# The even mixer of a two-layer transformer: its gated half's input tiles among the attention's steps

## What is computed

```python
q, k, v, bu, bv = jnp.split(z @ w_in, EVEN_SPLIT, axis=-1)
q = apply_rope_2d(rms_norm(q.reshape(b, s, A_HEADS, HEAD_DIM), q_gain), ang_r, ang_c)
k = apply_rope_2d(rms_norm(k.reshape(b, s, A_KV_HEADS, HEAD_DIM), k_gain), ang_r, ang_c)
...
y = jnp.concatenate([window_gqa(q, k, v, kc, vc, sink),
                     chunk_gmlp(bu, bv, v_gain, ws, bias)], axis=-1) @ w_out

def window_gqa(...):      # blocks of 128 queries; keys: previous, own, next block, and the context
    s_loc = jnp.where(valid, q.k * scale, NEG)
    p = softmax(concatenate([s_loc, s_ctx, s_sink]))
    o = p_loc @ v + p_ctx @ v_ctx

def chunk_gmlp(bu, bv, v_gain, ws, bias):
    u = jax.nn.gelu(bu)
    vv = rms_norm(jax.nn.gelu(bv)..., v_gain)          # per group of 64
    mixed = einsum('gij,bnjgd->bnigd', ws, vv) + bias  # per chunk of 128 tokens
    return u * mixed
```

## Time and profile before

| | us |
|---|---|
| median of 3 runs (3691.76 to 3694.46) | 3692.49 |
| the profiled execution | 3691.06 |
| its span in the profile | 3689.3 |
| its mean granted PE clock | 0.975 of 2.4 GHz |
| PE busy | 3540.4, 96% of the span |
| DVE busy | 2022.8, 55% |
| ACT busy | 983.9, 27% |
| even mixer, start of input tiles to start of output tiles | 630.60 to 993.62 |

### The profile page before, as it was taken

How to read it: one execution, slowest core, us unless ns; L and a number is a source line. 1 busy time by engine, 2 the same in 40 slices (tenths; PEclk the granted TensorE clock), 3 DMA queues, 4 the chain that set the end, 5 groups by cost and what they waited for, 6 DMA issues and landing times.

```text
span 3689.3 us, 45766 instructions
## 1 busy us (share of the span) xinstructions
PE 3540.4 (96%) x19352; PEld 3249.3 (88%) x19352; DVE 2022.8 (55%) x3166; ACT 983.9 (27%) x1442; POOL 18.2 (0%) x36
## 2 busy tenths in 40 slices
PE   6999999988899999999999999899999999999998
PEld 4999999976799999999999999777888878877777
DVE  6666645347657574456454455574333756455554
ACT  5112113134431111132111131443222432332232
POOL 0000000000000000000000000000000000000000
PEclk8999999988999999999999999899999999999999
DMA  5333422100023433113333122002222310111122
GB/s 199 126 126 124 132 70 78 65 12 4 25 68 116 135 115 101 59 65 128 126 123 98 60 98 70 17 34 83 97 96 93 126 57 13 64 67 55 51 91 80
DMA packets 86955, 308.53 MB, mean 84 GB/s; under 512 B 9856, under 2 KB 10048, under 8 KB 86368
## 3 DMA queue, kind: packets, MB, share of 16 engines
q1 hardware_dynamic: 82800, 290.04, 23.6%
q0 software_dynamic: 3952, 15.57, 1.2%
HBM read 301.38 MB, written 4.19 MB: 83 GB/s over the span
## 4 chain that ended last, share of the span: by engine, by line
PE 87%; DVE 8%; ACT 2%; issue 2%; DMA 1%; SPq 0%; ACTq 0%; DVEq 0%
PE psum L362 75%; PE psum L1188 2%; PE psum L1171 2%; PE psum L1179 1%; PE psum L993 1%; DVE nmx L1240 1%; DVE wl L355 1%; PE psum L1006 1%; ACT wh L345 1%; PE psum L2176 1%; PE psum L1728 1%; DVE ev_s L1237 1%; DMA raw<-in_ada_w 0%; PE psum L1737 0%; PE psum L2156 0%
## 5 line engine op out<-in xcount | busy, mean ns | idle before, releaser
L362 PE MATMUL psum<-zh,wh 128*128 128x384 f32 (+2 forms) x3792 | 1136.2, 358 | 33.7 <-DVE wl L355 12.3
L362 PE MATMUL psum<-zh,wl 128*128 128x384 f32 (+2 forms) x3792 | 1116.1, 353 | 0.0
L362 PE MATMUL psum<-zl,wh 128*128 128x384 f32 (+2 forms) x3792 | 1116.1, 353 | 0.0
L362 PEld LDWEIGHTS psum<-zh,wh 128*128 128x128 f32 x3792 | 701.1, 191 | 83.8 <-issue 22.5
L362 PEld LDWEIGHTS psum<-zl,wh 128*128 128x128 f32 x3792 | 702.2, 191 | 42.8 <-issue 4.6
L362 PEld LDWEIGHTS psum<-zh,wl 128*128 128x128 f32 x3792 | 701.2, 190 | 43.5
L345 ACT ACTIVATE wh<-raw 128x1024 fp32r<-128x1024 f32 (+2 forms) x431 | 437.1, 1022 | 978.4 <-PE psum L362 758.4
L355 DVE TENSOR_TENSOR wl<-raw,wh 128x1024 fp32r<-128x1024 f32 (+2 forms) x431 | 509.3, 1182 | 323.6 <-ACT wh L345 322.8
L688 DVE TENSOR_TENSOR scr<-psum,rf 128x768 f32<-128x768 f32 x132 | 126.4, 958 | 415.4 <-PE psum L362 415.4
L362 PE MATMUL psum<-hidh,wh 128*128 128x384 f32 (+1 forms) x1232 | 336.6, 342 | 0.0
L362 PE MATMUL psum<-hidh,wl 128*128 128x384 f32 (+1 forms) x1232 | 336.5, 342 | 0.0
(11 more groups left out here) (359 smaller groups left out, 2839.4 us busy)
## 6 DMA issues: line engine op xcount, KB each, us to landing
raw<-in_wup SPq DMA_DIRECT2D x176, 512.0 KB, 3.3
raw<-in_mod_w SPq DMA_DIRECT2D x128, 512.0 KB, 3.2
raw<-in_wdn SPq DMA_DIRECT2D x64, 448.0 KB, 3.3
raw<-in_w_sw SPq DMA_DIRECT2D x36, 512.0 KB, 3.2
raw<-in_wdn SPq DMA_DIRECT2D x32, 512.0 KB, 4.2
raw<-in_ada_w SPq DMA_DIRECT2D x16, 512.0 KB, 5.4
raw<-in_od_in SPq DMA_DIRECT2D x16, 512.0 KB, 3.2
raw<-in_w_ga SPq DMA_DIRECT2D x16, 512.0 KB, 3.3
```

The lines of the kernel that those rows point to most:

```text
L362: last = nc.tensor.matmul(psum[:, at + to:at + to + e - s], w[:, wslot(n), q * P:(q + 1) * P], x[:, q, s:e], start=(q == 0 and j == 0), st ...
```

## The change

Stage `ev_in` becomes two: `ev_qkv` (k, k, v, q, q, q, q: seven tiles) and `ev_uv` (vv 4, u 4). The seven run as before, with the sums of squares (L1378), the roots and the first rotation in the borders between tiles. The eight others are cut into their 64 chunks. Three or fewer chunks run in each of five turns, beside the remaining rotations, and then one or two after the scores in each step of the attention (`chunks_at`), which ends them in step 30. ACT and DVE do their share (gelu, square, gain, splits; drains, splits) at the same step in their own loops. All of `ev_uv` uses PSUM slot 0 (`alone`).

The query norm is no longer multiplied into q: its factor goes into the exponential as a scale per query row, its gain into the rotation matrix (`permqe`). The masks are added by PE: a product of the identity with `ev_mask` (L1638). DVE takes the maximum straight from PSUM. The lag is 1, there is one score buffer in PSUM and two probability buffers. The attention's output goes back into `ev`, and its high and low parts are made per head pair at the end. vv transposes are in steps 22 to 27, the mixing in steps 32 to 43, half a block at a time with one PSUM buffer (`VV_STEPS`, `MIX_STEPS`). The rows of `ev_out` are turned round so that the gated half comes first.

```diff
+        VV_STEPS = {22 + a: a for a in range(6)}
+        MIX_STEPS = {32 + s: s for s in range(12)}
+        def chunks_at(i):
+            return (1, 2, 1, 2, 2)[(i - 1) % 5] if i else 2
 PE, attention:
+            for i in range(NE + 2):
+                if i < NE:
+                    u = EUNITS[i]
+                    if i:
+                        pe.wait_ge(ea_e, i)
+                    for k, c, w in u.keys:
+                        masks = [m for m in u.masks if c <= m < c + w]
+                        last = nc.tensor.matmul(u.scores(c, w), u.q, k, start=True, stop=not masks)
+                        for m in masks:
+                            last = nc.tensor.matmul(u.scores(m, P), ident[:], ev_mask[:, min(m, P):min(m, P) + P],
+                                                    start=False, stop=True)
+                    last.then_inc(ea_qk, 1)
+                chunks_pe(pe, run, chunks_at(i))
+                if i in VV_STEPS:
+                    vv_rows_pe(pe, VV_STEPS[i])
+                if i in MIX_STEPS:
+                    mix_pe(pe, MIX_STEPS[i])
+                if 1 <= i <= NE:
+                    u = EUNITS[i - 1]
+                    pe.wait_ge(ea_p, i)
...
+                if i >= 2:
+                    u = EUNITS[i - 2]
+                    pe.wait_ge(ea_pc, i - 1)
...
 the mixing products wait for the step before:
+        def mix_pe(pe, s):
...
+            if s:
+                pe.wait_ge(mx_d, s)
 ACT, with a step's chunks:
+        def chunks_act(act, run, count):
+            for k in run.finished():
+                n, row = EU.n[k], ev[:, VVROW + k, :]
+                act.wait_ge(drained, DR[n])
+                if k < 4:
+                    link(act, "act", nc.scalar.activation(row, row, ACT.Gelu_apprx_tanh))
...
+                    nc.scalar.activation(esq[:, k % 2], row, ACT.Square).then_inc(v_sq, 1)
+                    nc.scalar.activation(row, row, ACT.Copy, scale=cols[:, BV + k:BV + k + 1]).then_inc(gelu_done, 1)
...
+            for s, k, q in run.take(count, True):
+                if q == 0:
+                    split_hi(act, s.n[k] + AHEAD)
 DVE, attention:
+            for i in range(NE + 2):
+                drains_dve(dve, run)
+                if i < NE:
...
+                    link(dve, "dve", nc.vector.reduce_max(m, u.scores(u.c0, u.w), AX.X))
+                    nc.vector.tensor_scalar(m, m, er[:, 48 + u.factor:49 + u.factor], nsinks[:, u.hd:u.hd + 1],
+                                            ALU.mult, ALU.min).then_inc(ea_s, 1)
+                if 1 <= i <= NE:
...
+                    nc.vector.tensor_scalar(u.probs(), u.probs(), rinv[:, r], None, ALU.mult).then_inc(ea_p, 1)
...
+                if i - 2 in MIX_STEPS:
+                    mix_low_dve(dve, MIX_STEPS[i - 2])
+                if i - 1 in MIX_STEPS:
+                    mix_dve(dve, MIX_STEPS[i - 1])
...
+                chunks_dve(dve, run, chunks_at(i))
```

More of the change, by code:

```diff
@@ L1286, in even_pool @@
             pool.dma_start(bbias[:], t["bbias"]).then_inc(ev_loaded, 16)
[L1287 removed]
+            pool.wait_ge(n_sum, 2)
             pool.dma_start(ev_mask[:], t["c_ev_mask"]).then_inc(ev_mask_in, 16)
             c_rows_pool(pool, 1)
[L1291 to L1317, removed]
[L1318 to L1321 removed]
@@ new lines, in drains_dve, with chunks_dve @@
+        def drains_dve(dve, run):
+            for k in run.finished():
+                drain_row(dve, EU, EU.n[k], ev[:, VVROW + k])
+                if k == 5:
+                    dve.wait_ge(v_root, 1)
+                    nc.vector.reciprocal(vr[:], vr[:]).then_inc(v_r, 1)
+        def chunks_dve(dve, run, count):
+            for s, k, q in run.take(count, True):
+                if q == 0:
+                    split_lo(dve, s.n[k] + AHEAD)
+                if q == s.chunks - 1:
+                    run.late.append(k)
@@ new lines, in even_dve @@
+            drain_to(dve, EQ, ev, norm=1, then=along)
+            run = Along(EU)
+            for turn in range(EV_TURNS):
+                drains_dve(dve, run)
+                if turn == 0:
+                    k_norm(dve, 1)
+                rope(dve, turn + 1)
+                if turn == 1:
+                    dve.wait_ge(v_tr, 1)
+                    for d in range(2):
+                        last = nc.vector.tensor_copy(vdup[:, :, :, d, :], psum[:, E_VT:E_VT + T]
+                                                     .rearrange("p (a g d) -> p a g d", a=6, g=2))
+                    last.then_inc(v_cp, 1)
+                if 1 <= turn <= 3:
+                    qk_factor(dve, turn + 2)
+                chunks_dve(dve, run, 3)
@@ L1422, in even_dve @@
+            heads_lo(dve, 3)
             dve.wait_ge(mod_done, 12)
@@ L1571, in build @@
         SM = 7
-        class Along:
-            def __init__(self, *stages):
-                self.units = [(s, k, q) for s in stages for k in range(s.tiles) for q in range(s.chunks)]
-                self.at, self.late = 0, []
-            def take(self, count):
-                self.at += count
-                return self.units[self.at - count:self.at]
-            def left(self):
-                return self.at < len(self.units)
         def along_pe(pe, run, count, then=None):
```

509 lines of the change are left out of this document (387 added, 122 removed).

## The result

| | us |
|---|---|
| before, median of 4 runs | 3693.03 |
| after, median of 4 runs | 3770.43 (3768.70 to 3771.62) |
| after / before | 1.0209, 95% interval 1.0197 to 1.0221 |
| span of the profiled execution after | 3766.9 |

The changed kernel is slower by 77 us. The direction was forecast, the size was not: 20 us were forecast, and 3770 lies above the range.

The account below looks back on a forecast made before the run. The prediction took PE to bound the mixer, with serial waits giving back what filling gains: 64.7 + 27 + 168.3 + 103.8 = 363.8 us against 363.0. Clock costs made it +20.8, span 3710, time 3713 us; range 3670 to 3745.

Parts of the forecast that it names:

- gelu steps: Steps 1, 6, 11, 16, 21, 26: PE waits behind ACT's table load, gelu and split and DVE's split; 28.9 us extra.
- mixing wait: Steps 33 to 43: PE's mixing products wait for DVE's product, about 3.5 us in eleven steps.
- ordinary division wait: In ordinary attention steps, transposes of probabilities wait 0.2 to 1.1 us for DVE's division.
- 12 us for six gelu steps: Low PE clock after gelu steps: 2 us each, bounds 0 and 4 (one step's work at half rate).
- 8 for the last 19 steps: Low clock in steps without chunks: 28% of 100 us, PE-bound for 0.3; upper bound all 48 us of PE work twice.
- the rival that the low clock holds in the last 19 steps: Attention's last 19 steps: 48 us of PE work doubled, 40 more than taken, 3753 us; chance 0.10.
- filled steps keep the clock up: Rival: chunks keep PE busy through waits, the 20 us of clock do not come, 3693 us; no change, chance 0.20.
- The masks: Six new mask products per head on PE, 6 x 0.22 = 1.4 us a head.
- Scores and P*V: PE work per attention head at full clock: scores 4.7 us, the 44 records of P*V 4.9 us.
- A chunk: One chunk of a weight tile on PE, priced 110.48/14/8 = 0.99 us.
- The start: Seven q, k, v tiles with borders, 64.7 us, and five turns, 27 us, ahead of the attention.
- The table drain: Rival: each of six table loads on the path also drains about 1.38 us, 8 us more, 3721 us; chance 0.07.

Follow-up runs that it names:

- e6: Changed kernel with vv transposes and mixing products behind P*V on PE, weight split ahead of gelu on ACT, division ahead of drain and maximum on DVE: 3676.4 us.
- e12: Changed kernel with unused PE products: eight of 256 columns behind each of six gelu steps, two of 512 columns in each of steps 32 to 48: 3721.4 us.
- e5: Changed kernel with two unused 512-column fp32 products on PE in each of steps 32 to 48: 3737.8 us.
- e8: Changed kernel with eight unused 256-column fp32 products on PE in each of steps 2, 7, 12, 17, 22 and 27: 3751.4 us.
- e4: Changed kernel without the 48 mask products of the scores on PE: 3742.4 us.
- e11: Changed kernel with a plain copy in place of each of the eight gelus, and the table loads around them gone: 3751.0 us.

## Why the prediction was right and where it was wrong

**The direction and its reason: right.** The prediction said that what filling gains, the serial steps give back. With the three orders changed, +77 us becomes -15 (e6). Each of the three is worth 21 to 32 us by itself, clock included.

**The waits: right in kind, the gelu steps too high.** The mixing wait was forecast about 3.5 us eleven times and is 3.43. The ordinary division wait was forecast 0.2 to 1.1 and is 0.69 where one chunk covers it. The gelu step was forecast at "some 5" and is 3.83 in the step shown, 4.7 at the longest. Its chain from the table load to the end of the split is 767.40 - 761.34 = 6.1 us, as priced (6.6 less the 0.45 of the output copy). The six waits together are 4.24 + 3.83 + 4.39 + 4.71 + 2.79 + 3.20 = 23.2 us, where the sum had 28.9 beyond the ordinary wait: at least 6 too much.

**The clock: the step that failed.** The sum took 12 us for six gelu steps and 8 for the last 19 steps, 20 in all. The runs show 49 us and more: e12 gives 49 back although it does 50 us of work beside, some 9 of them outside the waits. So the low clock's cost is estimated at 49 to 58 us. The mis-sized term was in two places. For the last steps, "28% of their 100 us" was carried over from the attention before, where the waits were 1.4 us. The new steps had waits of 3 us in nine, and the clock was 0.64 and 0.59, so most of the 48 us of PE work ran at half rate. In e5 the same steps have a clock of 0.98. The sum's own bound, "all 48 us of PE work twice", and the rival that the low clock holds in the last 19 steps describe what happened there: e5 gives 33 us back, the rival had 40. The rival's chance was 0.10, and its 3753 falls short too, since it left the gelu steps at 12 us. For the gelu steps, 2 us was taken as half the work of one step. The dip goes on for about ten us after the wait (770 to 780 at 0.50), while PE is busy nearly all the time, and so more than one step's work runs at half rate. e8 finds 19 us and more for six of them, 3 us and more each: inside the bounds of 0 and 4, above the 2 that was taken.

The Trainium skill (TensorE: Matmul & The Clock Gate, section HAM oscillation — how this bites in real kernels) tells of a kernel in which every short burst of products is followed by a wait, there for a DMA, so that each burst starts at the low level again. By that rule, the trace agrees: burst, wait of 3.1 to 3.8 us, burst, at a mean clock of 0.64. The prediction used section What's actually happening of the same page of the Trainium skill, for the rival that filled steps keep the clock up. In steps 0 to 31 PE was shown busy for 176.78 of 208.10 us, 0.85, no more than in the attention before (134.28 of 158.00), and their mean clock is 0.87 where that had 0.86.

**The masks: a second mis-sized term.** 1.4 us a head, priced from rows of products of one kind; they are 2.55 a head at full clock, so 20.4 instead of 11.5 us. The alternation of 64-row and 128-row products was visible in the order of the changed kernel. No row that the prediction used has its price, but the trace of before does: two score records of 256 columns take 0.63 us until the transposes begin, not 0.43.

```profile
850.61 0.70 PE L1171 MATMUL psum<-ev 64*128 64x256 f32 x2
851.24 0.77 PE L1179 MATMUL psum<-ident,ev_s 128*128 128x128 f32 x5
```

**Scores and P*V: a little dear too.** At full clock a head's scores without masks, each up to the chunk that follows, are 1.07 + 1.28 + 1.28 + 1.06 + 0.62 + 0.62 = 5.9 us in e4, where 4.7 was priced. P*V up to the next scores is 0.54, 0.99 and 1.21 us for 4, 8 and 10 records (760.41, 755.84 and 750.27), 5.5 a head against 4.9. That is 1.8 a head, at most 14 us over eight, since some of it can lie under a wait.

**A chunk: wrong by its divisor.** 110.48 us in the earlier trace rows are 624 records, 13 tiles of 48 and not 14, so a chunk is 110.48/13/8 = 1.06 and not 0.99. For 50 chunks in steps 0 to 30 this is 3.5 us.

**The start: 4.7 too long.** The first scores come at 717.62 instead of 722.3. It is the same divisor: eight tiles of 8.50 and not 7.89 leave 54.1 us for the other seven and not 59.0, and the 14 chunks of the turns take 1 us more.

**The table drain: did not happen.** The gelu starts at 762.64, 0.02 us after its load ends (761.34 + 1.28). The Trainium skill (ScalarE: Activation LUTs, section What ACT_TABLE_LOAD costs) adds a drain of about 1.38 us to each switch; no run here shows it. In e11, without the load, the wait is 1.42 us shorter. The load's own 1.28 and the drain of that page of the Trainium skill would together be 2.7, as an estimate.

**The account.** The mixer came out 55.6 us above the forecast of 383.8. The clock is 29 to 38 of it, the masks 9, the chunks 3.5, the start -4.7, the gelu waits -6. That makes 31 to 40. The scores and P*V can give up to 14 of the 16 to 25 us that are left, which was not tested alone; the rest is not assigned. Two of the errors pull the other way, 11 us together, and by luck hid as much of the others.

## What to carry to other kernels

Where short bursts of TensorE alternate with waits like those here (3.1 to 3.8 us in steps of 9 to 11), price the work behind each wait at the low clock, not at a mean taken from a stage with shorter waits. When work of a background stage is laid between dependent steps, look in every in-order queue at what it pushes back: here the split stood behind a gelu, the division behind a maximum and the transposes behind a mixing product, and none of them had to. A cheap proof that the clock is the cause is to add unused work in the gaps: if the kernel becomes faster, it is.

## What the runs showed of the hardware that was not expected

- Unused PE work made the kernel faster: 29 us of it gave 33, 21 us gave 19, both together 49.
- After a wait of 3.83 us PE stayed at its low level for about 10 us of almost uninterrupted work (clock 0.50 from 770 to 780, PE busy for 9.85).
- A 128-row fp32 product of 128 columns takes 0.42 us between two 64-row products and 0.24 before one of its own kind. Grouping them gave 9.6 us without changing any product.
- With the waits of e6 short (2.1 us at most for the mixing), the clock returned without filling: 0.92 in 900 to 960.
